# A two-layer decoder step on one core: memory scores over the full array height, an earlier first weight tile, a third split place, and five waits in other places

## What is computed

```python
def mem_attend(q, k, v):                       # 4 heads of 64, 256 memory rows
    s = jnp.einsum('bthd,bmhd->bhtm', q, k).astype(F32) * (MEM_HD ** -0.5)
    p = jax.nn.softmax(s, axis=-1).astype(v.dtype)
    return jnp.einsum('bhtm,bmhd->bthd', p, v)
...
# layer 0: z = rmsnorm(h) @ w_in -> q, k, v, gate of 6 retention heads, memory queries
#          h += concat(retention * silu(gate), mem_attend) @ w_out;  h += relu(rmsnorm(h) @ w_up)^2 @ w_down
# between: one compressed latent c and one rotary key for layer 1
# layer 1: the same with latent attention (6 heads; 8 samples over 2048 cached rows) in place of retention
```

## Time and profile before

| | before |
|---|---|
| three runs | 1559.57, 1560.48, 1561.18 us (median 1560.48) |
| the profiled execution | 1561.1 us, span 1559.3 us |
| mean granted TensorE clock | 0.993 |
| PE busy | 1527.9 us (98%) |
| DVE busy | 804.6 us (52%) |
| ACT busy | 575.5 us (37%) |
| POOL busy | 49.3 us (3%) |
| DMA | 149.74 MB, mean 96 GB/s |

### The profile page before, as it was taken

One profiled execution on the slowest core, in us unless ns is written; L12 is line 12 of the kernel. 1 busy time (PEld: TensorE's weight loads), 2 busy tenths in 40 slices (PEclk: granted clock), 3 DMA queues, 4 the chain that ended last, 5 costly groups with the idle time before them and its releaser, 6 DMA issues.

```text
span 1559.3 us, 28925 instructions
## 1 busy us (share of the span) xinstructions
PE 1527.9 (98%) x11519; PEld 1419.7 (91%) x11519; DVE 804.6 (52%) x1275; ACT 575.5 (37%) x904; POOL 49.3 (3%) x74
## 2 busy tenths in 40 slices
PE   7999999999999999999998999999999999999998
PEld 6998888899999999999998567667999999999998
DVE  3857777655434334344577456655454343343444
ACT  6633333234313223133444265554343132231333
POOL 1110000010000000000001000000000000000000
PEclk8999999999999999999999999999999999999999
DMA  8363222342222223222334415523222223322221
GB/s 255 115 200 83 81 78 79 92 146 81 83 82 82 82 87 86 85 82 82 82 82 121 121 44 146 148 74 98 72 82 82 82 82 88 88 82 82 82 82 61
DMA packets 231407, 149.74 MB, mean 96 GB/s; under 512 B 11297, under 2 KB 225074, under 8 KB 231282
## 3 DMA queue, kind: packets, MB, share of 16 engines
q1 hardware_dynamic: 219746, 123.86, 28.1%
q0 software_dynamic: 5968, 20.18, 4.4%
q10 hardware_dynamic: 5568, 3.93, 0.9%
HBM read 140.26 MB, written 7.68 MB: 95 GB/s over the span
## 4 chain that ended last, share of the span: by engine, by line
PE 91%; DVE 5%; ACT 1%; issue 1%; DMA 1%; ACTq 0%; SPq 0%; DVEq 0%
PE ps L635 72%; PE ps L1246 3%; PE ps L1120 3%; PE ps L1273 2%; PE ps L1216 1%; PE ps L1179 1%; PE ps L1180 1%; DVE t L2265 1%; PE ps L1099 1%; DVE wl L1862 1%; DVE onorm L2061 1%; PE ps L1102 1%; DMA raw<-in_a_w_in 1%; DVE gn L2055 0%; PE ps L1197 0%
## 5 line engine op out<-in xcount | busy, mean ns | idle before, releaser
L1361 ACT ACTIVATE wh<-raw 128x1024 fp32r<-128x1024 f32 (+1 forms) x195 | 202.1, 1036 | 606.1 <-PE ps L635 597.7
L635 PE MATMUL ps<-xh,wh 128*128 128x288 f32 x1542 | 335.8, 299 | 5.2 <-DVE wl L1862 4.7
L635 PE MATMUL ps<-mh,wh 128*128 128x288 f32 (+1 forms) x1424 | 323.0, 295 | 6.8 <-DVE wl L1862 3.6
L635 PE MATMUL ps<-xh,wl 128*128 128x288 f32 x1542 | 328.8, 295 | 0.0
L635 PE MATMUL ps<-xl,wh 128*128 128x288 f32 x1542 | 328.7, 295 | 0.0
L635 PE MATMUL ps<-mh,wl 128*128 128x288 f32 (+1 forms) x1424 | 321.2, 294 | 0.0
L635 PE MATMUL ps<-ml,wh 128*128 128x288 f32 (+1 forms) x1424 | 321.1, 294 | 0.0
L1862 DVE TENSOR_TENSOR wl<-raw,wh 128x1024 fp32r<-128x1024 f32 (+1 forms) x195 | 233.0, 1195 | 73.0 <-ACT wh L1361 71.2
L635 PEld LDWEIGHTS ps<-xh,wh 128*128 128x128 f32 x1542 | 246.7, 189 | 15.2 <-issue 7.2
L635 PEld LDWEIGHTS ps<-xl,wh 128*128 128x128 f32 x1542 | 247.7, 189 | 0.0
L635 PEld LDWEIGHTS ps<-xh,wl 128*128 128x128 f32 x1542 | 247.6, 189 | 0.0
(11 more groups left out here) (323 smaller groups left out, 1290.9 us busy)
## 6 DMA issues: line engine op xcount, KB each, us to landing
raw<-in_w_up SPq DMA_DIRECT2D x64, 512.0 KB, 4.0
raw<-in_w_down SPq DMA_DIRECT2D x64, 512.0 KB, 4.0
pages<-in_cache_mla SPq DMA_DIRECT2D x128, 160.0 KB, 2.2
raw<-in_a_w_in SPq DMA_DIRECT2D x26, 512.0 KB, 4.1
memkc<-in_cache_mem_k POOLq DMA_DIRECT2D x16, 256.0 KB, 6.0
memvc<-in_cache_mem_v POOLq DMA_DIRECT2D x16, 256.0 KB, 6.1
raw<-in_a_w_out SPq DMA_DIRECT2D x8, 512.0 KB, 4.5
raw<-in_b_w_out SPq DMA_DIRECT2D x8, 512.0 KB, 4.8
```

Of the source, the lines that this page charges most:

```text
L635: last = mm(ps[:, 2 * (m % 2) + c, 0:n], w[:, s, kk, :], x(kk, col, n), start=(kk == 0 and nth == 0), stop=(kk == final and nth == 2))
L1361: do(f(wh[:, m % 2, 0:k, :], raw[:, m % NRAW, 0:k, :], ACT.Copy), C[whi_ready])
```

## The change

- Both matmuls of a score run over all 128 partitions. The first takes `kT` with its upper 64 partitions set to zero, the second a copy `odd_keys` with its lower 64 set to zero. The semaphores between the halves are gone; `keys_apart` says that the zeroed keys are there. In layer 0 `memory_tile` writes the copy from PSUM; in layer 1 DVE does a memset, a copy and a memset at item k = 5 of the key and value items.
- The two M_Q weight tiles are issued by ACT, behind the first and the third block of x.
- Tile M_OUT[0] + 2 gets split places of its own (`wh_apart`, `wl_apart`, in the space of x's last blocks) and is split during the last retention head.
- Waits and order: `r_lo` in the last head; `w_tail(109)` behind `add_squares`; `w_tail(110)` ahead of the four 32-row multiplications; `w_head` and `w_tail` of M_OUT[1] ahead of the last unit's values on ACT and DVE; the second half of M_OUT[1] + 1's left half behind L1316 on PE.

```diff
+        wh_apart = sb("wh_apart", [P, KD, P], F32R, A_XH + 6 * TILE)
+        wl_apart = sb("wl_apart", [P, KD, P], F32R, A_XL + 6 * TILE)
+        def split(m):
+            return (wh_apart, wl_apart) if m == M_OUT[0] + 2 else (wh[:, m % NSPLIT, :, :], wl[:, m % NSPLIT, :, :])
...
 # SP, the start
-            for j in range(2):
-                sp.dma_start(raw[:, M_Q + j, :, :], wcols(wa, 4 * RET_W + P * j)).then_inc(w_loaded[M_Q + j], 16)
 # ACT, the start, in the loop over the blocks n of x
+                if n % 2 == 0:
+                    act.dma_start(raw[:, M_Q + n // 2, :, :], wcols(t["a_w_in"][0], 4 * RET_W + P * (n // 2))).then_inc(w_loaded[M_Q + n // 2], 16)
...
 # PE, layer 0 (layer 1 alike, with keys_apart 2 and odd_keys[1])
-                mm(ps[:, 7, 0:256], qm[0:64, b, P * i:P * i + P], kT[0:64, 0, b, :], start=True, stop=True).then_inc(me_half, 1)
+                pe.wait_ge(keys_apart, 1)
+                mm(ps[:, 7, 0:256], qm[:, b, P * i:P * i + P], kT[:, 0, b, :], start=True, stop=True)
-                pe.wait_ge(me_half, u + 1)
-                mm(ps[:, 7, 256:512], qm[64:P, b, P * i:P * i + P], kT[64:P, 0, b, :], start=True, stop=True).then_inc(me_sc, 1)
+                mm(ps[:, 7, 256:512], qm[:, b, P * i:P * i + P], odd_keys[0][:, b, :], start=True, stop=True).then_inc(me_sc, 1)
...
 # PE, the last head
-            pe.wait_ge(r_lo, last)
+            pe.wait_ge(r_lo, last - 1)
             out_part(0, 0, 1, 2)
             ret_scores(last)
+            pe.wait_ge(r_lo, last)
             out_part(0, 3, 4)
...
 # PE, the end of the attention
-            dense(M_OUT[1] + 1, tiles(mh), tiles(ml), half=0)
+            dense(M_OUT[1] + 1, tiles(mh), tiles(ml), half=0, part=range(KD // 2))
...
             last.then_inc(uv_ps, 1)
+            dense(M_OUT[1] + 1, tiles(mh), tiles(ml), half=0, part=range(KD // 2, KD))
             out_and_mlp(1)
...
 # ACT
+                if m == M_OUT[0] + 2:
+                    act.wait_ge(acc_ready, M_OUT[0])
...
             ret_rows(last)
+            w_head(M_OUT[0] + 2)
             root_table()
...
-            unit_values(UNITS - 1)
             act.wait_ge(l_pv, chunk_step(13) + 1)
             w_head(M_OUT[1])
+            unit_values(UNITS - 1)
...
 # DVE
+                if j < 2:      # memory_tile
+                    do(tt(odd_keys[0][64:P, j, :], ps[64:P, 2 * (m % 2), 0:NMEM], rmem[64:P, :], ALU.mult))
...
+            do(dve.memset(odd_keys[0][0:64, :, :], 0.0))
...
             dve.wait_ge(consts_in, 16 * 8)
+            dve.wait_ge(kv_rows_ps, 2)
+            do(dve.memset(kT[64:P, 0, :, :], 0.0), C[keys_apart])
...
+            ret_kv(last)
+            w_tail(M_OUT[0] + 2)
+            ret_update(last)
...
 # DVE, rotary (r is set for tile 108 alone)
                 do(tt(halves(t1[:, :]), acc(m), halves(ropeCb[:, :]), ALU.mult))
+                if between is not None and r is not None:
+                    w_tail(between)
                 for a in range(4):
...
                     scaled(m, cT[:, m - M_KV, :], rstd[:, :])
-                    w_tail(m + 2)
+                    if m == M_KV:
+                        w_tail(m + 2)
                     add_squares(4 if m == M_KV else None)
+                    if m > M_KV:
+                        w_tail(m + 2)
...
+                if k == 5:
+                    dve.wait_ge(acc_ready, M_OUT[1])
+                    dve.wait_ge(kv_rows_ps, 6)
+                    do(dve.memset(odd_keys[1][0:64, :, :], 0.0))
+                    do(copy(odd_keys[1][64:P, :, :], kT[64:P, 1, :, :]))
+                    do(dve.memset(kT[64:P, 1, :, :], 0.0), C[keys_apart])
...
             probs(CHUNKS - 1)
+            w_tail(M_OUT[1])
             unit_values(UNITS - 1)
-            w_tail(M_OUT[1])
```

More of the change, by code:

```diff
@@ L376, in build @@
         ab_ps, l_q = sem("ab_ps"), sem("l_q")
-        u_half, u_sc, u_max, u_exp, u_norm, u_tr, u_pt, u_pv, u_hi, u_lo = (
-            sem(f"u_{n}") for n in ("half", "sc", "max", "exp", "norm", "tr", "pt", "pv", "hi", "lo"))
+        u_sc, u_max, u_exp, u_norm, u_tr, u_pt, u_pv, u_hi, u_lo = (
+            sem(f"u_{n}") for n in ("sc", "max", "exp", "norm", "tr", "pt", "pv", "hi", "lo"))
         pg_in = [[sem(f"pg_in{n}_{bb}") for bb in range(2)] for n in range(5)]
@@ L627, in dense @@
                         pe.wait_ge(acc_free, at(freed(m - 1), i))
-                s = m % NSPLIT
+                head, tail = split(m)
                 cols = ((0, 0),) if n != HALF else ((0, 0), (1, HALF)) if half is None else ((half, HALF * half),)
@@ L632, in dense @@
                         pe.wait_ge(ready[0], ready[1](kk))
-                    for nth, (w, x) in enumerate(((wh, hi), (wh, lo), (wl, hi))):
+                    for nth, (w, x) in enumerate(((head, hi), (head, lo), (tail, hi))):
                         for c, col in cols:
-                            last = mm(ps[:, 2 * (m % 2) + c, 0:n], w[:, s, kk, :], x(kk, col, n),
+                            last = mm(ps[:, 2 * (m % 2) + c, 0:n], w[:, kk, :], x(kk, col, n),
                                       start=(kk == 0 and nth == 0), stop=(kk == final and nth == 2))
@@ L1163, in unit_half @@
                 i, b = q // 2, q % 2
-                mm(ps[:, q % 2, 0:256], qm[0:64, b, P * i:P * i + P], kT[0:64, 1, b, :], start=True, stop=True).then_inc(u_half, 1)
+                pe.wait_ge(keys_apart, 2)
+                mm(ps[:, q % 2, 0:256], qm[:, b, P * i:P * i + P], kT[:, 1, b, :], start=True, stop=True)
             def unit_scores(q):
@@ L1173, in unit_scores @@
                     i, b = q // 2, q % 2
-                    pe.wait_ge(u_half, q + 1)
-                    last = mm(ps[:, q % 2, 256:512], qm[64:P, b, P * i:P * i + P], kT[64:P, 1, b, :], start=True, stop=True)
+                    last = mm(ps[:, q % 2, 256:512], qm[:, b, P * i:P * i + P], odd_keys[1][:, b, :], start=True, stop=True)
                 else:
@@ L1357, in w_head @@
                 act.wait_ge(w_loaded[m % NRAW], at(loaded_value[m], i, 16 * LAP // NRAW))
-                if m >= 2 or i is not None:
+                if m == M_OUT[0] + 2:
+                    act.wait_ge(acc_ready, M_OUT[0])
+                elif m >= 2 or i is not None:
                     act.wait_ge(acc_ready, at(m - 1, i))
                 k = k_tiles(m)
-                do(f(wh[:, m % 2, 0:k, :], raw[:, m % NRAW, 0:k, :], ACT.Copy), C[whi_ready])
+                do(f(split(m)[0][:, 0:k, :], raw[:, m % NRAW, 0:k, :], ACT.Copy), C[whi_ready])
             def squares(src, n=ROWS):
@@ L1616, in out_and_mlp @@
                 for j in range(KD):
-                    w_head(M_OUT[layer] + j + 2)
+                    if layer or j:
+                        w_head(M_OUT[layer] + j + 2)
                     act.wait_ge(acc_free, freed(M_OUT[layer] + j + 1))
@@ L1850, in do @@
                 dve.wait_ge(count.sem, count.value())
-            C = {s: Count(s) for s in (wlo_ready, acc_free, diag_ready, scale_taken, sq_used, mem_lo, x_lo, h_lo,
+            C = {s: Count(s) for s in (wlo_ready, acc_free, keys_apart, diag_ready, scale_taken, sq_used, mem_lo, x_lo, h_lo,
                                        me_max, me_norm, me_lo, ms_q, ms_max, ms_o, ms_lo, r_dve, r_masked, r_st, r_state, r_var, r_norm, r_mix, r_lo,
@@ L2202, in _ @@
             w_tail(M_OUT[0] + 1)
-            for step in (ret_rows, ret_scores, ret_kv, ret_update, ret_out, ret_back):
-                step(last)
+            ret_rows(last)
+            ret_scores(last)
+            ret_kv(last)
+            w_tail(M_OUT[0] + 2)
+            ret_update(last)
+            ret_out(last)
+            ret_back(last)
             def add_residual(m, j, i=None):
@@ L2212, in out_and_mlp @@
                     add_residual(M_OUT[layer] + j, j)
-                    w_tail(M_OUT[layer] + j + 2)
+                    if layer or j:
+                        w_tail(M_OUT[layer] + j + 2)
                     add_squares((2, 6)[layer] if j == 0 else None)
@@ L2267, in rotary @@
                     inside()
-                if between is not None and between < M_OUT[1]:
+                if between is not None and r is None and between < M_OUT[1]:
                     w_tail(between)
```

5 lines of the change are left out of this document (3 added, 2 removed).

## The result

Four runs of the changed kernel took 1548.98 to 1550.30 us, median 1549.62; the kernel before, beside them, 1560.03. The ratio is 0.9933, with a 95% interval from 0.9919 to 0.9947: faster by 10.4 us. I had said 1547.7, between 1542.5 and 1553.0. The profiled execution took 1550.3 us with a span of 1548.2; PE was busy for 1517.9 us (98%), DVE for 808.0 and ACT for 575.7.

The account below looks back on a forecast made before the run. TensorE (PE), at 91%, was taken as the bound. The terms 3.4 + 2.4 + 1.5 + 0.6 + 1.65 + 1.6 - 0.8 + 2.4 = 12.8 us off 1561.1, less 0.6, gave 1547.7 us; range 1542.5 to 1553.0.

Parts of the forecast that it names:

- a shared array: Rival, score matmuls: the 64-row halves ran side by side, so full height wins nothing; 1560.4 us, no change; chance 0.03.
- twice the passes: Rival, 32 score matmuls: full-height float32 scores take twice the passes, each 0.43 us more; 1567.3 us; chance 0.02.
- Layer 0's scores: Layer 0 memory scores: 0.40 us off each isolated 64-row matmul, 2.8 in part 2 and 0.6 in part 0; 3.4 us won.
- Layer 1's scores: Layer 1 memory scores: drains cost 0.66 us a unit, four laps with units gain; 2.4 us won.
- the clock gives back more: Rival: the 1.2 GHz stretch behind 894.9 halves and the start's shrinks by 3.4 us; 1544.3 us; chance 0.14.
- The start: Kernel start: M_Q tile lands earlier behind one block of x; 1.5 us won, bounds +2.1 and -2.1.
- ACT's queue blocks: Rival, kernel start: the start gains nothing or loses 0.6 us instead of winning 1.5; 1549.2 to 1549.8; chance 0.18.
- r_lo: Last retention head: PE's old wait for ml goes, but L837 must then wait for vexp; 0.6 us won.
- The third place: Tile 36, last retention head: with the split done before, PE's 1.77 us wait for wl mostly goes; 1.65 us won.
- The 1.6 for the clock: Behind the gap at tile 36: the 3.4 us at 1.2 GHz go with PE busy there; 1.6 us won (0 or 1.7).
- Tiles 107 to 110: Tiles 107 to 110: w_tail(109) behind add_squares makes everything behind later; 0.8 us lost, between 0 and -0.8.
- The end of the attention: M_OUT[1]: its 1.17 us wait goes, the second of 1.30 gets work under it; 2.4 us won (bounds 1.2 and 2.5).

Follow-up runs that it names:

- scores_only: The kernel before with only the scores changed to 128 partitions, everything else as before; median 1553.19 us against 1559.77 beside it.
- no_third: The changed kernel without the third split place, tile M_OUT[0] + 2 split in the two old places; median 1550.53 us.
- start_sp2: The changed kernel with SP issuing both M_Q tiles, the second only after block 1 of x has landed; median 1550.09 us.
- after_again: The changed kernel, unchanged, timed and profiled once more on the same chip; median 1549.92 us.

## Why the prediction was right, and where not

The forecast lay 1.9 us under the measured time. That it came so near is in part luck: the start missed by more than that one way and the clock in layer 1 by more than that the other way, and the two nearly cancel. The rivals of a shared array and of twice the passes fell with the 0.39 us won on each isolated score.

- **Layer 0's scores: 3.4 forecast, 2.5 measured.** The 0.40 off each isolated matmul is right (0.39). Between the `ret_back`s of the heads 0.72, 0.61, 0.58, 0.56 and 0.04 us were won, where I had 0.70, three times 0.85, and 0.15. Head 1 came as forecast: the two scores of part 2 gave 0.78, and 0.05 of it was lost again in the wait for DVE's `onorm`. The step that failed is 0.40 off each of the two in the heads behind it. There the first score of part 2 waits for the `ml` of the unit before it, in both kernels:

```profile
160.67 0.29 PEld L728 LDWEIGHTS ps<-kT,qm 64*128 64x128 f32 x2 [0.26 <-DVE ml L1982]
```
```profile
160.83 0.30 PEld L735 LDWEIGHTS ps<-kT,qm 128*128 128x128 f32 x2 [0.26 <-DVE ml L1998]
```

It starts 0.45 us behind the dense pair ahead of it, before (160.22 to 160.67) and after (160.38 to 160.83). So what a 64-row matmul loses ahead of itself was hidden under this wait, only what it loses behind itself goes, and part 2 gives 0.58. Part 0 left 0.06 instead of 0.15 behind the wait for `krow` (a gap of 0.22 now), and the wait for `onorm` took back 0.04 (0.18, before 0.14).

- **Layer 1's scores: 2.4 forecast, 2.25 measured**, and beside it the stretch at 1.2 GHz that cost 2.5. I had left it in ("the wait of 1.73 us stays"); the wait did stay, the stretch didn't. The rival "the clock gives back more" had this place right in kind (it took half of the stretch, all of it went) and the start wrong.
- **The start: 1.5 won forecast, 1.5 lost measured**; the sign was wrong. The bounds held (-2.1), and the rival "ACT's queue blocks" had it in kind, but not in size. The step that failed is "I take 1.1 for the two new ones and 0.5 more behind ... nearer the good end because the queue holds less here": the issues ran until 11.41 instead of 6.52, 4.9 us more, near my 5.2 for the bad end. ACT's head then started at 14.40, where that end had 14.7. My own sign for being wrong, a table load behind 10, came true.
- **r_lo: 0.6 and 0.60.** The new wait is `vexp`'s, 0.66 long. `scores_only`, without this part, shows it once more: 29.14 us from 287.25 to 316.39, against 28.52.
- **The third place: 1.65 and 1.55.** PE still waits 0.22 for `res`. The 1.6 for the clock came as well (1.97 from tile 36 to `stats(18)`, less the 0.43 that `stats(18)` waits less). But my reason, that PE is busy in place of the gap, is not shown: `no_third` and `scores_only` have the gap of 1.77 and no stretch behind it. The size is right by luck as far as the runs tell.
- **Tiles 107 to 110: -0.8 and -0.94**, with the mechanism as told.
- **The end of the attention: 2.4 and 2.73**, read from the comparison alone, since no run takes this part back by itself (`scores_only`, which lacks it, has both waits). 1.24 for the wait on M_OUT[1], and 1.49 for the split of the sample values, at PE's half of M_OUT[1] + 1:

```profile
1081.77 2.79 PE L1323 MATMUL ps<-ols,uvs 128*128 128x64 f32 x24
1084.36 0.38 PE L641 MATMUL ps<-mh,wh 128*128 128x288 f32 x1
```

- **Not in the sum:** 1.03 lost in the profiled execution on ACT's issue of uv, by chance.

Against the profiled spans (11.1 won of 12.8): the start 2.45 too high, layer 0 0.9, uv 1.0; the clock in layer 1 2.5 too low.

## What to carry to other kernels

A matmul over half the partitions between full ones costs its neighbours time (0.39 us here); zero the other half of the operand if that is cheap. Look for a wait that stands right ahead of it already, which hides a part of that cost, and for what waits next, before you count all of it. A transfer moved to an engine that computes is paid for by that engine where its issues are held up: count what it has issued already, put transfers in the order in which they are needed, and hold back the late ones with a wait on an idle engine. Work that fills an engine's wait for another engine is free there; moved behind the wait, it delays all that follows, by up to the length of the wait.

## What the runs showed of the hardware that I had not expected

- The first six issues on ACT took 0.5 to 0.8 us each, but for one of 1.2 and one of 1.6; behind some 2.2 MB of x and weights issued there one took up to 3.0 us. Over all profiled executions seven issues at the start ended at 6.5 to 6.7, eight at 6.3 to 7.2, ten at 10.5 to 11.4. The Trainium skill, DMA: Bandwidth & Descriptors, Rules for kernel authors, says that spreading DMAs over engines gives no bandwidth and only saves issue time. The bandwidth didn't change here either (270 to 279 GB/s from 4 to 15 us in five kernels with four different starts), but which engine issues, and in which order, moved PE's first dense product from 16.09 to 12.23 and its gap from 36.58 to 32.99.
- PE's clock fell to 1.2 GHz twice behind gaps of 1.7 us in both profiled executions of the kernel before, and behind the same gaps in other kernels sometimes not at all. The shortest gap with a stretch behind it was 1.30 us (`scores_only`), and behind 1.94 there was none in `scores_only` and `start_sp2`. One such stretch of 3.4 us cost 1.3 (layer 1), 1.5 (tile 36) and 1.4 us (`scores_only`), the one of 6.9 us 2.5.
- The clock's record can miss the start: the changed kernel's first profile shows 1.00 where four transposes take 1.12 us, `after_again` 0.50 in the same place. At full speed they take 0.60 to 0.66, so the durations tell the clock there. In the kernel before, the four at 5.47 took 1.11 where 1.00 is shown, so its slow time at the start was longer than the 10.2 us that I had read from the earlier trace rows.
